# Gate tiles in three rotating rows, a weight split moved ahead of two gate pieces, and five key tiles scored as three and two

## The reference, cut to what matters

```python
p = jnp.einsum('btd,dc->btc', rmsnorm(x) , w_in)              # 1088 rows x 1024 -> many column groups

# short gated convolution, 256 channels = two halves of 128
y_conv, new_buf = short_conv(p['conv_c'] * p['conv_h'], conv_buf, W['conv_w'][l])
o_conv = p['conv_b'] * y_conv * jax.nn.silu(p['conv_z'])

# attention of the prompt, per block of 128 queries, 2 kv heads x 4 query heads
p_s = masked_softmax(jnp.einsum('bqhgd,bqhkd->bqhgk', qs, kv_sel[..., 0, :]), m_s)   # selected keys
o_s = jnp.einsum('bqhgk,bqhkd->bqhgd', p_s.astype(dt), kv_sel[..., 1, :])
p_w = masked_softmax(jnp.einsum('bqhgd,bkhd->bqhgk', qs, kv_band[:, :, 0]), m_w)     # last 512 keys
o_w = jnp.einsum('bqhgk,bkhd->bqhgd', p_w.astype(dt), kv_band[:, :, 1])
return gates[..., 0:1] * o_c + gates[..., 1:2] * o_s + gates[..., 2:3] * o_w
```

## Time and profile before

| | us |
|---|---|
| median of three runs | 944.85 (943.0 to 945.55) |
| the profiled execution's own time | 942.26 |
| its span, first to last instruction | 940.5 |
| PE busy | 885.2 (94%) |
| DVE busy | 589.7 (63%) |
| ACT busy | 423.9 (45%) |
| POOL busy | 203.2 (22%) |

### The profile page before, as it was taken

How to read it: one execution, slowest core, us unless ns; L and a number is a source line. 1 busy time by engine, 2 the same in 40 slices (tenths; PEclk the granted TensorE clock), 3 DMA queues, 4 the chain that set the end, 5 groups by cost and what they waited for, 6 DMA issues and landing times. The chain is left out here.

```text
span 940.5 us, 16467 instructions
## 1 busy us (share of the span) xinstructions
PE 885.2 (94%) x5775; PEld 774.2 (82%) x5775; DVE 589.7 (63%) x1392; ACT 423.9 (45%) x942; POOL 203.2 (22%) x220
## 2 busy tenths in 40 slices
PE   5999999998998999999999999997788999999997
PEld 4999999998998999888899988885355767777665
DVE  6432110148344567899877679996477688787663
ACT  6432221110104565778755667774453345444322
POOL 0019599999804000000000015000000000000000
PEclk9999999999998999999999999997789999999999
DMA  7226644443304221000011010434334464551411
GB/s 252 78 90 185 266 158 133 148 153 112 114 1 136 65 59 40 16 1 1 1 47 50 22 46 17 120 103 152 113 104 122 130 207 144 155 165 43 145 53 35
DMA packets 106819, 93.72 MB, mean 100 GB/s; under 512 B 21245, under 2 KB 99954, under 8 KB 104626
## 3 DMA queue, kind: packets, MB, share of 16 engines
q1 hardware_dynamic: 84946, 58.65, 20.7%
q10 hardware_dynamic: 19488, 17.25, 5.9%
q0 software_dynamic: 2304, 16.78, 5.1%
HBM read 78.16 MB, written 18.61 MB: 103 GB/s over the span
## 5 line engine op out<-in xcount | busy, mean ns | idle before, releaser
L680 PE MATMUL ps<-w_hi,h_hi 128*128 128x264 f32 (+5 forms) x432 | 123.9, 287 | 0.2 <-DVE h_lo L552 0.2
L680 PE MATMUL ps<-w_lo,h_hi 128*128 128x264 f32 (+5 forms) x432 | 122.8, 284 | 0.0
L680 PE MATMUL ps<-w_hi,h_lo 128*128 128x264 f32 (+5 forms) x432 | 122.8, 284 | 0.0
L560 DVE TENSOR_TENSOR w_lo<-w_raw,w_hi 128x1024 fp32r<-128x1024 f32 (+3 forms) x13 | 35.3, 2718 | 126.7 <-ACT w_hi L454 126.7
L1549 DVE TENSOR_REDUCE least<-ps 128x1 f32<-128x640 f32 (+7 forms) x128 | 89.7, 703 | 18.7 <-PE ps L1358 17.1
L1479 ACT ACTIVATE pt_hi<-ps 128x512 fp32r<-128x512 f32 x132 | 78.6, 598 | 45.0 <-PE ps L1375 41.2
L1553 DVE TENSOR_TENSOR pt_lo<-ps,pt_hi 128x512 fp32r<-128x512 f32 x132 | 89.8, 686 | 10.0 <-ACT pt_hi L1479 8.6
L401 POOL TENSOR_TENSOR chunk<-chunk 128x1024 f32<-128x1024 f32 (+2 forms) x46 | 81.5, 1771 | 3.6
L680 PEld LDWEIGHTS ps<-w_hi,h_hi 128*128 128x128 f32 (+1 forms) x432 | 79.6, 184 | 0.5 <-issue 0.4
L680 PEld LDWEIGHTS ps<-w_lo,h_hi 128*128 128x128 f32 (+1 forms) x432 | 79.5, 184 | 0.0
L680 PEld LDWEIGHTS ps<-w_hi,h_lo 128*128 128x128 f32 (+1 forms) x432 | 79.3, 184 | 0.0
(11 more groups left out here) (385 smaller groups left out, 2225.4 us busy)
## 6 DMA issues: line engine op xcount, KB each, us to landing
kv_pages<-in_cache_slc_kv SPq DMA_DIRECT2D x256, 64.0 KB, 1.9
shared<-in_x_prompt SPq DMA_DIRECT2D x8, 512.0 KB, 3.6
w_raw<-in_w_in SPq DMA_DIRECT2D x8, 512.0 KB, 4.0
wr_raw<-in_w_in SPq DMA_DIRECT2D x8, 512.0 KB, 4.0
kv_window<-in_cache_win_kv SPq DMA_DIRECT2D x4, 1024.0 KB, 5.4
wo_raw<-in_w_out SPq DMA_DIRECT2D x8, 512.0 KB, 8.3
out<-in_cache_win_kv SPq DMA_DIRECT2D x1, 4032.0 KB
x_row<-in_x_prompt ACTq DMA_DIRECT2D x7, 512.0 KB, 5.1
```

What stands on the lines that cost most here:

```text
L560: nc.vector.tensor_tensor(half(w_lo, b), raw(b), half(w_hi, b).bitcast(F32), ALU.subtract).then_inc(s_wlo, 1)
L680: mm = nc.tensor.matmul(out, lhs, rhs, start=(k == 0 and i == 0), stop=(k == KD - 1 and i == 2))
```

## The change

Three edits. The buffer `tanh` goes; the tanh of gate piece n is written into row n mod 3 of `stage`, which earlier in the stage holds rows on their way to DRAM. The first three pieces wait for those stores, the later ones until VectorE is done with piece n - 3. On VectorE, the weight split of block b + 2 now stands behind the first taken piece of a z block instead of the third. And scores of five tiles are made of three and two tiles instead of four and one; the three begin at column 128 of their bank, so that the 640 scores stay contiguous for VectorE and ScalarE. The planner's table gets the same pieces, so its lists change for the whole stage.

```diff
-        tanh = sb("tanh", [P, 2, 364])
...
                         n = gate_no[x]
-                        if n >= 2:
-                            wait_taken(act, gates[n - 2])
-                        nc.scalar.activation(tanh[:, n % 2, 0:tn], ps[:, bank(x), 0:tn], ACT.Tanh, scale=0.5
+                        if n >= 3:
+                            wait_taken(act, gates[n - 3])
+                        else:
+                            act.wait_ge(s_st[n], 16 * ((len(staged) - n + 2) // 3))
+                        nc.scalar.activation(stage[:, n % 3, 0:tn], ps[:, bank(x), 0:tn], ACT.Tanh, scale=0.5
...
-                    if b >= NTB:
-                        for x in prods:
-                            if x[0] == b and taken[x][0] == "dve":
-                                take(x)
+                    mine = [x for x in prods if x[0] == b and taken[x][0] == "dve"]
+                    first = 1 if kind(b) == "z" else len(mine)
+                    for x in mine[:first]:
+                        take(x)
                     if b + 2 < NB:
                         split(b + 2)
+                    for x in mine[first:]:
+                        take(x)
...
+    def pieces(tiles):
+
+        cut = 3 if tiles == 5 else 4
+        return [(c, min(cut, tiles - c), (4 - cut) * P if c == 0 else 0) for c in range(0, tiles, cut)]
...
-            chunks = [min(512, n - c) for c in range(0, n, 512)]
+            chunks = [P * count for _, count, _ in pieces(tiles_of[x])]
...
         def S(g, n):
-            return ps[:, 2 * (g % 2):2 * (g % 2) + 2, :].rearrange("p a b -> p (a b)")[:, 0:n]
+            at = pieces(n // P)[0][2]
+            return ps[:, 2 * (g % 2):2 * (g % 2) + 2, :].rearrange("p a b -> p (a b)")[:, at:at + n]
...
-                        for c in range(j0, j1 + 1, 4):
-                            n = min(4, j1 + 1 - c) * P
-                            bank = 2 * (y % 2) + (c - j0) // 4
+                        for m, (c, count, to) in enumerate(pieces(tiles_of[x])):
+                            c, n, bank = c + j0, count * P, 2 * (y % 2) + m
                             edge = c == j0 and br == 1 and i >= WIN // P
-                            nc.tensor.matmul(ps[:, bank, 0:n], q_hi[:, i % 2, y * P:(y + 1) * P],
+                            nc.tensor.matmul(ps[:, bank, to:to + n], q_hi[:, i % 2, y * P:(y + 1) * P],
                                              kT[:, br, c * P:c * P + n], start=True, stop=False)
```

More of the change, by code:

```diff
@@ L589, in take @@
                         dve.wait_ge(s_tanh, n + 1)
-                        did(nc.vector.scalar_tensor_tensor(tanh[:, n % 2, 0:tn], tanh[:, n % 2, 0:tn], 1.0, src,
+                        did(nc.vector.scalar_tensor_tensor(stage[:, n % 3, 0:tn], stage[:, n % 3, 0:tn], 1.0, src,
                                                            ALU.add, ALU.mult))
                         nc.vector.scalar_tensor_tensor(y_t[:, t0:t0 + tn], y_t[:, t0:t0 + tn], 0.5,
-                                                       tanh[:, n % 2, 0:tn], ALU.mult, ALU.mult
+                                                       stage[:, n % 3, 0:tn], ALU.mult, ALU.mult
                                                        ).then_inc(s_td, 1)
@@ L1351, in _ @@
                             pe.wait_ge(s_mask, masked(x))
-                        for c in range(j0, j1 + 1, 4):
-                            n = min(4, j1 + 1 - c) * P
-                            bank = 2 * (y % 2) + (c - j0) // 4
+                        for m, (c, count, to) in enumerate(pieces(tiles_of[x])):
+                            c, n, bank = c + j0, count * P, 2 * (y % 2) + m
                             edge = c == j0 and br == 1 and i >= WIN // P
-                            nc.tensor.matmul(ps[:, bank, 0:n], q_hi[:, i % 2, y * P:(y + 1) * P],
+                            nc.tensor.matmul(ps[:, bank, to:to + n], q_hi[:, i % 2, y * P:(y + 1) * P],
                                              kT[:, br, c * P:c * P + n], start=True, stop=False)
                             mm = nc.tensor.matmul(
-                                ps[:, bank, 0:n].rearrange("p (t c) -> p t c", c=P),
+                                ps[:, bank, to:to + n].rearrange("p (t c) -> p t c", c=P),
                                 q_lo[:, i % 2, y * P:(y + 1) * P],
@@ L1362, in _ @@
                             if edge:
-                                mm = nc.tensor.matmul(ps[:, bank, 0:P], ident_r[:, :], pen_r[:, :], start=False,
+                                mm = nc.tensor.matmul(ps[:, bank, to:to + P], ident_r[:, :], pen_r[:, :], start=False,
                                                       stop=True)
```

## The result

| | before, us | change, us | ratio |
|---|---|---|---|
| at first: median of 4 and 4 runs | 944.17 | 932.41 (930.82 to 933.51) | 0.9874 (0.9856 to 0.9892) |
| repeated, 15 and 5 runs | 944.63 | 934.73 (930.12 to 937.27) | 0.9895 (0.9869 to 0.9921) |
| repeated again, 11 and 6 runs | 943.5 | 933.58 (930.18 to 936.56) | 0.9901 (0.9869 to 0.9934) |
| the profiled execution's own time | 942.26 | 933.51 | |
| its span | 940.5 | 931.7 | |

The kernel is 11.8 us faster by the first comparison, against 7.95 predicted. The ratio is estimated from all the runs with a 95% interval. The two profiled executions are only 8.75 us apart.

What follows compares the result with a forecast made beforehand. TensorE was taken to set the pace in projections and attention, with VectorE close behind in the attention. Savings of 5.46 and 2.5 us, set as 8.0 against a median of 944.85, gave 936.9; range 933.5 to 942.0.

Steps and rivals of the forecast that it cites:

- The projections: Before block 10, TensorE's wait for `w_lo` and the clock dip behind it both go: 5.46 us saved.
- The attention, widths: Five-tile heads cut as three and two save 3.6 us at most; 2.5 taken, as VectorE is close behind.
- The part that each head saves: In the attention, 0.05 to 0.10 us less for each of 32 heads with an edge, 0.05 for 8 without.
- The part that is given back: In the attention, VectorE lags and TensorE waits for `pt_lo`; two more such waits give back 1.2 us.
- The attention, order: The planner's new order of the whole attention stage: taken as zero, with TensorE's 2.5 us of idle as bound.
- the only term for the clock: Where the projections end, TensorE's wait may lose 1.5 or 3.4 us to a lower clock: 1.9 either way.
- given back to VectorE: Rival in the attention: VectorE takes back the whole gain, 939.4 us; 0.21 together with time by columns.
- Time by columns: Rival in the attention: matmul time goes by columns alone, so the new cut saves nothing: 939.4 us, chance 0.05.
- The new waits: Rival in the attention: more TensorE waits for `pt_lo`, 0.59 us each; 948.7 us with 20 more; chance 0.14.
- GpSimd does hold the split: Rival in the projections: GpSimd's multiply holds VectorE's split, TensorE waits 1.43 us; 938.3 us, chance 0.15.

Runs made afterwards that it cites:

- the widths alone: Five-tile scores cut as three and two, with the planner's old costs and the old projections, against the kernel before: 940.84 us, ratio 0.9961.
- the split alone: Weight split moved behind the first gate piece, two tanh buffers kept, attention of before, against the kernel before: 939.55 us, ratio 0.9939.
- the first joint filled: On top of the change, 4 extra matmuls behind the projections' last product and 12 ahead of the attention's first step: 929.94 us, ratio 0.9854 to the kernel before.

## Why the prediction missed

**The projections: right.** 5.46 was the price of the wait with its dip, 5.37 to 5.45 is what three profiles of the change show and 5.33 what the edits bring alone. The split took 1.75 against bounds of 1.23 and 3.36, and the two late gate pieces and the split of block 11 (done at 233.89, wanted at 239.5) made no wait.

**The attention, widths: right in sum, wrong in parts.** 2.5 was forecast and 2.41 measured. The part that each head saves was taken too large (0.10, measured 0.05 in the head, its lower end, and 0.08 with what follows): the edge kept its 0.06, but the matmul behind it took 0.05 more. The part that is given back was too large as well (1.1, measured 0.5, in waits for VectorE as forecast). That the two errors cancel is luck. By the formula for two single matmuls in the Trainium skill (TensorE: Matmul & The Clock Gate, "Back-to-back issue gap") the two ways to cut would cost the same; the widths alone, 2.41 us shorter from the first score to the last, say that they do not.

**The attention, order: a mis-sized term.** "The new order of the whole stage has no price of its own in the trace ... I take zero." It brought about 1.0, half of it out of the idle time that the prediction had named as its bound. With 5.4 and 2.4 that makes the 8.8 by which the last oT and the profiled span are earlier, against 8.0 forecast.

**The failing step: how a gain in one trace becomes a median, and what the range has to hold.** The prediction set 8.0 off against the median of three runs, and the only term for the clock in its range stood for one joint: "Where the stage ends ... that is 1.9 us either way". At that joint the profile of before and the three of the change show the same 6.8 us of half clock. The spread is elsewhere and larger. All 55 executions of the kernel before that were timed took 939.52 to 949.38 us, median 944.39, and the mean granted clock falls with the time: 0.980 in those near 939.8, 0.973 near 945.0, 0.968 near 949.3. The 15 of the change took 930.12 to 937.27, median 933.51, at 0.984 to 0.971. A change of 0.01 in the mean clock goes with about 7 us.

So the 4.5 us between forecast and result are: 0.8 from the mechanism (8.8 instead of 8.0); 0.5 from the base (944.85 of three runs, 944.39 of 55); 1.1 from the four runs of the change, which were a low draw (932.41 against 933.51 of 15, which is the low end of the range almost to the digit, so that the first median fell outside is in part the draw); and 2.1 that are left, 944.39 - 933.51 - 8.8. The three profiles of the change end 291.2 to 294.7 behind the last oT and that of before 294.7, so the spread of the tail is large enough to hold such a rest. The mean clocks say that most of it goes with the clock: they average 0.9781 over the 15 executions of the change and 0.9739 over 51 of the kernel before. Some 0.0018 of the difference is the dip of 3.4 us at block 10 (half of 3.4 in 940), whose price is in the 8.8 already; the other 0.0024, at 7 us for 0.01, is some 1.7 us of the 2.1 (an estimate). That the change made the tail's clock better is not shown: the timed executions leave no trace, and the other kernels here took 294.1 to 299.2 for the tail. Why the clock was higher stays open.

**The rivals.** Of the 2.9 that the heads saved, 0.5 were given back to VectorE with the widths alone, not all. Time by columns fell with the widths alone as well. The new waits did not cost anything: 8 for `pt_lo`, as before, more for `prob_slc`, and between the first score and the last TensorE idles 2.37 us, before 2.35. GpSimd does hold the split, but only where it starts late, as the split alone showed. On that the Trainium skill (SBUF — State Buffer, "Who interferes with whom") has the port held by whoever issues first. Here VectorE's instruction had started first each time and was held all the same: by 0.40 in the kernel before, 0.40 in the change (224.32 and 224.72) and 0.34 with the split alone (223.75 and 224.09). In each it ended behind the multiply. So the order of the starts does not tell here who waits. The rows show starts and not issues, and the profile's spans of GpSimd are rough, so how the two share the port stays open.

**Better than both** is the change with the first joint filled: 929.94 against 933.58 for the change beside it, and 3.2 us by landmarks that are ahead of the tail.

## What to carry to other kernels

Where a weight split waits behind other work, look for every cause that stands in line: here a third row for the tanh alone and an earlier place for the split alone brought nothing and 4.2 of 5.4 us, since each left the other's delay. Cut a row of key tiles so that no piece is only 128 columns wide: here such a piece took 0.11 us, hardly less than the 0.12 of 256 columns. Before a gain of some microseconds is set off against a median, look at how the mean clock and the time of single executions go together, and give the range that spread as a term; where TensorE stands still at a joint, try idle matmuls in front of the next stage: here they were worth 3.2 us at one joint, more than the new widths, and nothing at the other.

## What was not expected of the hardware

- A VectorE instruction of 0.5 to 1.2 us that starts up to 0.40 us ahead of GpSimd's multiply of 128x2048 (3.66 us) is held until behind its end: it took 4.46, 4.47 and 5.08 us.
- The same kernel's tail took 291.2, 293.5 and 294.7 us in three profiles, with all landmarks ahead of it the same to 0.2 us.
- 16 extra matmuls (4 and 12) in a pause of 3.95 us kept the granted clock at 1.00 over the next 10 us, where it was 0.75, and moved what follows, up to the last oT, by 3.2 us.
- The edge matmul of 128 columns takes 0.06 us between wide ones, but a 256-wide matmul behind it takes 0.17 instead of 0.12.
